# Sample attention of a decoder layer: two phases in a row against eight steps side by side

## The chip, the core and the metric

The program runs on one core of a Trainium2 chip. Five engines work there from queues of their own and meet at semaphores: TensorE (PE in the rows, and PEld for its weight loads) multiplies, VectorE (DVE) and ScalarE (ACT) work on what lies in the on-chip memories, GpSimd (POOL) subtracts here, and SyncE (SP) starts most transfers. The metric is the device time of one execution in microseconds (us), as the median over runs. The kernel before takes 1402.89 us (median of 3 runs, 1401.07 to 1404.97).

## The reference

One layer of a decoder: an input projection, two kinds of mixing, an output projection and a layer norm. There are 512 prompt tokens, and 8 samples with 4 new tokens each, behind 1024 cached positions. Cached keys and values lie in pages of 128 positions, 8 pages for a sample, 512 KB a page and kind. What matters here, cut from the reference (L is 1028, topk 256, 8 heads of width 128):

```python
def _sample_attention(l, q, k_new, v_new, qi, ki_new, wi, cache_k, cache_v, cache_kidx, page_table):
    ...
    _, idx = lax.top_k(scores, topk)
    valid = idx <= qpos[None, :, None]
    ...
    k_sel = jnp.where(is_past, cache_k[l, phys_page, offset].astype(k_new.dtype), k_new[bidx, nidx])
    v_sel = jnp.where(is_past, cache_v[l, phys_page, offset].astype(v_new.dtype), v_new[bidx, nidx])
    return _sparse_attend(q, k_sel, v_sel, valid)

def _pool_mix(u_ext, n_hist, w_pool, pool_scale):
    # trailing means over 2, 4, 8, 16 tokens minus the token, for four groups of 256 channels,
    # then a 256 x 256 map for each group
    ...
def _combine(x, a, p, ga, gb, w_out, ln_g, ln_b):
    mixed = jnp.concatenate([a.reshape(B, T, ATTN_WIDTH) * jax.nn.silu(ga),
                             p * jax.nn.silu(gb)], axis=-1)
    h = (DEEPNORM_ALPHA * x + jnp.einsum('btc,cd->btd', mixed, w_out)).astype(jnp.float32)
    ...
```

The kernels read every page and put a mask over the scores in place of the gather: positions that were not picked get -1e30 ahead of the softmax.

## The kernel before

The kernel runs through stages A (indexer), C (attention of the prompt, head by head), B (attention of the samples, and pooling) and D (output projection and norm). The change lies in stage B, lines 788 to 870 (ScalarE), 1122 to 1281 (TensorE), 1549 to 1632 (VectorE) and the transfers in `group` on SyncE (lines 445 to 516). Stages A, C and D stay as they are.

**Tiles and quarters.** A projection turns 2048 inputs into 128 output columns for 544 tokens. Such a tile is two units of weights (512 KB each), and a unit is two quarters: `quarter` is 24 matmuls on line 922, six for each of four chunks of inputs (high and low parts of weights and activations). Weights land in `rawW`, ScalarE rounds them into `wH` (`high`), GpSimd takes the difference into `wL` (line 558). Two accumulators in PSUM, `acc0` and `acc1`, take turns from tile to tile, so that a finished tile is copied out while the next one is computed. Stage B has four groups, and each has four tiles (two for the pooling input U, two for its gate) and two samples, a and b.

**One sample.** First the keys: in 16 steps `turned(n)` transposes four 128 by 128 blocks of key pages into bank 4 or 5 (line 1139), VectorE (even n, line 1562) or ScalarE (odd n, line 593) copies them into `kPT`, and `products(n)` multiplies them by the sample's queries (line 1155), two heads side by side in two of the four 32-column strips of the array. Three quarters stand between those steps. Then come the new keys, two quarters, and the transposes of the probabilities (lines 1186 and 1189) once the softmax is through on VectorE and ScalarE. Then the values: `value_pages` takes the eight pages in two lots of four (line 1200, eight heads in four strips), with a quarter between, and after the last quarter the output is turned (line 1230). When both samples are done, the map of the pooling group follows (line 1280).

**What sets the order.** All queues are written out by hand and each runs strictly in its order. Bank use is a table: `Banks.stage` deals names out over banks in turn, and a use waits until the one before it in the same bank was read. Bank 4 and 5 serve keys, probabilities, history rows, outputs and the pooling map; banks 6 and 7 serve scores and the value sums. `vPage` has 4 slots of one page, and SyncE starts a page's transfer when TensorE has freed its slot (`v_free`). `kPage` has 2 slots of two pages. SyncE's order in a group is: pooling inputs, weights, key pages, two value pages, weights, key pages, mask, two value pages, weights, and the other four value pages behind one another.

## Time and profile before

| what | value |
|---|---|
| median of 3 runs | 1402.89 us (1401.07 to 1404.97) |
| profiled execution: its time, its span | 1407.33 us, 1405.5 us |
| TensorE busy | 1281.5 us, 91% of the span |
| VectorE, ScalarE, GpSimd busy | 587.0, 361.7 and 350.6 us (42%, 26%, 25%) |
| matmuls of the projections (line 922) | 7008 records, 508.6 + 491.9 + 491.9 us |
| stage B | 690.0 to 1173.6 us |
| stage D | from 1176.0 us |
| granted TensorE clock over the span | 0.955 of 2.4 GHz |
| DMA over the span | 170.67 MB, mean 121 GB/s |

The profile shows one execution. Busy times of TensorE add up the records, which overlap, so that a start-to-start distance in the timeline says more than a record's duration. "Idle before" names what ended a wait. Line numbers are those of the kernel that was run.

### The profile page before, as it was taken

How to read it: one execution, taken by the hardware profiler on the slowest of the kernel's cores; microseconds unless marked ns; L12 is line 12 of the kernel's file. 1: busy time of each engine (PE TensorE's matmuls, PEld its weight loads, DVE VectorE, ACT ScalarE, POOL GpSimd, SP SyncE). 2: the span in 40 equal slices, each digit the busy share in tenths (PEclk: the TensorE clock that was granted, in tenths of full speed). 3: DMA queues.
4: the chain of work that ended last, by engine and by line, in shares of the span. 5: the costliest groups of instructions: out<-in, count | busy, mean ns of one | idle time of the engine just before them, and what ended most of it. 6: DMA issues, size and time to landing. Idle time of an engine off the chain costs nothing. (4 is left out here: it accounts for less than half of the span.)

```text
span 1405.5 us, 27397 instructions
## 1 busy us (share of the span) xinstructions
PE 1281.5 (91%) x10300; PEld 1128.3 (80%) x10300; DVE 587.0 (42%) x1079; ACT 361.7 (26%) x663; POOL 350.6 (25%) x150
## 2 busy tenths in 40 slices
PE   7899968898999999899898998988989898999995
PEld 6777758898999999899776767757677677999993
DVE  3555588973084066137431323313132234222226
ACT  4223231223223123223321222212222123212210
POOL 2322202422433243243211212202120121434320
PEclk9999978999999999999999999999999999999996
DMA  8423121322332233234247465464736646422203
GB/s 245 115 72 82 33 73 54 85 78 60 91 98 69 73 102 83 62 92 121 86 147 263 160 198 180 141 219 142 245 121 195 212 140 200 137 83 81 88 2 128
DMA packets 197987, 170.67 MB, mean 121 GB/s; under 512 B 19890, under 2 KB 178538, under 8 KB 196658
## 3 DMA queue, kind: packets, MB, share of 16 engines
q1 hardware_dynamic: 184458, 160.48, 37.3%
q10 hardware_dynamic: 13424, 8.67, 2.2%
q8 instruction: 80, 1.31, 0.4%
q14 instruction: 25, 0.20, 0.0%
HBM read 159.47 MB, written 9.74 MB: 120 GB/s over the span
## 5 line engine op out<-in xcount | busy, mean ns | idle before, releaser
L558 POOL TENSOR_TENSOR wL<-rawW,wH 128x1024 fp32r<-128x1024 f32 (+1 forms) x146 | 350.4, 2401 | 1006.6 <-ACT wH L579 1006.6
L922 PE MATMUL acc<-actH,wH 128*128 128x272 f32 (+1 forms) x2336 | 508.6, 300 | 11.6 <-issue 8.2
L922 PE MATMUL acc<-actH,wL 128*128 128x272 f32 (+1 forms) x2336 | 491.9, 293 | 0.0
L922 PE MATMUL acc<-actL,wH 128*128 128x272 f32 (+1 forms) x2336 | 491.9, 293 | 0.0
L922 PEld LDWEIGHTS acc<-actH,wH 128*128 128x128 f32 (+1 forms) x2336 | 375.5, 193 | 37.4 <-issue 35.4
L922 PEld LDWEIGHTS acc<-actL,wH 128*128 128x128 f32 (+1 forms) x2336 | 376.9, 193 | 0.0
L922 PEld LDWEIGHTS acc<-actH,wL 128*128 128x128 f32 (+1 forms) x2336 | 373.6, 193 | 0.0
L579 ACT ACTIVATE wH<-rawW 128x1024 fp32r<-128x1024 f32 (+1 forms) x146 | 153.9, 1055 | 300.3 <-PE acc L922 278.0
L1562 DVE COPY kPT<-bank 128x512 f32<-128x512 f32 x64 | 44.2, 691 | 176.3 <-PE bank L1139 176.3
L1139 PEld LDWEIGHTS bank<-sq,kPage 128*128 128x128 f32 x512 | 56.0, 144 | 53.9 <-issue 50.5
L1155 PE MATMUL bank<-kPT,qPad 128*32 128x256 f32 x512 | 81.9, 399 | 13.0 <-DVE kPT L1562 6.6
L1139 PE MATMUL bank<-sq,kPage 128*128 128x128 f32 x512 | 85.5, 293 | 5.0 <-issue 5.0
L593 ACT ACTIVATE kPT<-bank 128x512 f32<-128x512 f32 x64 | 38.2, 597 | 140.3 <-PE bank L1139 139.6
L1653 DVE SCALAR_TENSOR_TENSOR y<-y,bank 128x512 f32 x16 | 11.0, 688 | 135.0 <-PE bank L1290 125.9
L1484 DVE SCALAR_TENSOR_TENSOR gate<-tanhC,raw 128x544 f32<-128x544 f32 x8 | 5.8, 723 | 144.7 <-ACT raw L770 144.7
L1384 DVE SCALAR_TENSOR_TENSOR scoreP<-relu,wiN,scoreP 128x256 f32<-128x256 f32 (+2 forms) x54 | 38.8, 753 | 63.9 <-ACT relu L636 63.9
L1200 PE MATMUL bank<-vPage,probST 128*4 128x128 f32 x1024 | 35.9, 276 | 23.3 <-DMA vPage<-in_cache_v 23.3
L1622 DVE SCALAR_TENSOR_TENSOR mixed<-bank,gateS 128x32 f32 x8 | 1.5, 192 | 129.2 <-PE bank L1230 129.2
L636 ACT ACTIVATE relu<-bank 128x512 f32<-128x512 f32 (+3 forms) x63 | 29.2, 504 | 87.5 <-PE bank L979 71.9
L1200 PEld LDWEIGHTS bank<-vPage,probST 128*4 128x4 f32 x1024 | 23.5, 87 | 33.1 <-DMA vPage<-in_cache_v 30.3
L1155 PEld LDWEIGHTS bank<-kPT,qPad 128*32 128x32 f32 x512 | 18.8, 109 | 38.4 <-issue 25.5
L979 PE MATMUL bank<-kiT,raw 64*128 64x256 f32 (+2 forms) x108 | 32.0, 587 | 15.3 <-DVE qiN L1398 11.7
(193 smaller groups left out, 988.4 us busy)
## 6 DMA issues: line engine op xcount, KB each, us to landing
rawW<-in_w_in SPq DMA_DIRECT2D x112, 512.0 KB, 3.8
kPage<-in_cache_k SPq DMA_DIRECT2D x64, 512.0 KB, 5.2
vPage<-in_cache_v SPq DMA_DIRECT2D x64, 512.0 KB, 5.2
rawW<-in_w_out SPq DMA_DIRECT2D x32, 512.0 KB, 3.9
y<-in_x_prompt SPq DMA_DIRECT2D x4, 1024.0 KB, 8.1
out_y_prompt<-y SPq DMA_DIRECT2D x8, 512.0 KB, 2.8
xnat<-in_x_prompt SPq DMA_DIRECT2D x2, 1024.0 KB, 7.7
xnat<-in_x_prompt ACTq DMA_DIRECT2D x2, 1024.0 KB, 11.3
```

The lines of the kernel that those rows point to most:

```text
L558: pool.tensor_tensor(wL[:, slot, :, 0:width], rawW[:, slot, :, 0:width], wH[:, slot, :, 0:width].bitcast(F32), ALU.subtract).then_inc(stag ...
L579: act.activation(wH[:, t.slot, :, 0:width], rawW[:, t.slot, :, 0:width], ACT.Copy).then_inc(high_ready[t.slot], 1)
L593: act.activation(dst, src, ACT.Copy).then_inc(bank_free[b.slot], 1)
L636: act.activation(relu[0:rows, t.slot, 0:n], src[0:rows, 0:n], ACT.Relu).then_inc(relu_full[t.slot], 1)
L922: last = pe.matmul(acc[t.slot][0:width, e, 0:HT], w[:, u.slot, k, 0:width], a[:, kk, e * HT:(e + 1) * HT], start=(kk == 0 and w is wH and ...
L979: full(b, pe.matmul(take(b)[:, 0:(t + 1) * P], raw[part, slot, t * P:(t + 1) * P], kiT[part, 0:(t + 1) * P], start=True, stop=True))
L1139: last = pe.transpose(dst[:, (2 * e + a) * P:(2 * e + a + 1) * P], kPage[:, 1 - k.slot, a, 2 * hp + e, :], ident)
L1155: last = pe.matmul(bank[st.slot][at:at + SPAN, pair % 2 * 256:pair % 2 * 256 + 256], qPad[:, X, h * NS:(h + 1) * NS], kPT[:, n % 2, e, :], ...
L1200: return pe.matmul(bank[o.slot][j * SPAN:j * SPAN + NT, a * P:(a + 1) * P], probs, values, start=start and a == 0, stop=stop and a == HALF ...
L1384: dve.scalar_tensor_tensor(sc, relu[:, r.slot, 0:(t + 1) * P], wiN[:, t - 1, ds(h, 1)], sc, ALU.mult, ALU.add).then_inc(bank_free[b.slot], 1)
L1562: dve.tensor_copy(kPT[:, 0, :, :].rearrange("p h k -> p (h k)"), bank_wait(dve, b)[:]).then_inc(bank_free[b.slot], 1)
L1653: dve.scalar_tensor_tensor(at, at, ALPHA, bank_wait(dve, b)[:].rearrange("p (t c) -> p t c", t=TT), ALU.mult, ALU.add).then_inc(bank_free[ ...
```

## The change

Stage B becomes a pipeline over samples. A sample's eight value pages run beside the next sample's keys in eight steps, m = 0 to 7. In step m TensorE transposes the keys of step m + 1 (eight blocks, banks 4 and 5), may run a quarter, multiplies the keys of step m (four heads in four strips, `key_products`), and takes value page m of the sample before (`value_page`). Pieces:

- The keys of the first sample run ahead of the loop with quarters 0 to 4. The loop runs three times over two samples, "b" beside the values of "a", and "c" (the next group's "a") beside the values of "b". The last group is written out behind it, and its last eight value pages have no keys beside them.
- All tiles of the stage use `acc1` (`tile_turn`). The two halves of `acc0` become banks: OUT (8) for the sums over values, SIDE (9) for history rows, last rows, new keys, the third part of the probabilities, outputs and the pooling map. In the rows a wait on them is bank_free8 and bank_free9.
- Transposed keys have a second place, two rows of `mixed` that are still unused then (`key_slot`). The output is copied into `probST` instead of `probS`, so the mask of the next sample can be loaded after the probabilities are turned.
- SyncE starts each value page four steps ahead and each pair of key pages three steps ahead; two more tiles of output weights are loaded within the last group instead of behind it.
- On VectorE the window sums (line 1591), gates and pooling results are cut up and stand between the key copies. On ScalarE the copies of projections, `high` and the last rows do.

The diff, cut: bank tables, SyncE's order, TensorE's order, and for the first sample of a group the orders of ScalarE and of VectorE.

```diff
+def tile_turn(tile, i=None, per=0):
+    if tile < TILE_B:
+        slot, n, step = tile % 2, tile // 2, per // 2
+    elif tile < TILE_D:
+        slot, n, step = 1, TILE_B // 2 + tile - TILE_B, per
+    else:
+        slot, n, step = (tile - TILE_D) % 2, (tile - TILE_D) // 2, per // 2
+        n += TILE_B // 2 + (KC if slot else 1)
+    return Turn(slot, n if i is None else i * step + n)
...
-            outS = probS[:, 0:HALF * P].rearrange("p (a d) -> p a d", a=HALF)
+            outS = probST[:].rearrange("p a t -> p (a t)").rearrange("p (a d) -> p a d", a=HALF)
+            def key_slot(n):
+                if n // 2 % 2:
+                    return mixed[:, KC - 2 + n % 2, 0:4 * P]
+                return kPT[:, n % 2, :, :].rearrange("p h k -> p (h k)")
...
+        OUT, SIDE = 8, 9
+        bank[OUT], bank[SIDE] = acc[0][:, 0, :], acc[0][:, 1, :]
...
+        def beside_keys(X, Y):
+            return [*key_uses(Y, 0, 2), f"Pt0{X}", f"Pt1{X}", *key_uses(Y, 2, 16)]
+        side = ["h0", "Pt2a", "h1", "u0", "u1", "Snb", "OTa", "Pt2b", "m0p", "m0s", "m1p", "m1s"]
+        LOOPS = GROUPS - 1
+        stages = []
+        for names in ((key_uses("a"), ["S0a", "S1a"], ["Sna"], []),
+                      (beside_keys("a", "b") + beside_keys("b", "c"), ["S0b", "S1b", "S0c", "S1c"],
+                       [*side, "Snc", "OTb"], ["Oa", "Ob"]),
+                      (beside_keys("a", "b") + ["Pt0b", "Pt1b"], ["S0b", "S1b"], [*side, "OTb"], ["Oa", "Ob"])):
+            times = LOOPS if len(stages) == 1 else 1
+            stages.append([banks.stage(n, w, times) for n, w in zip(names, ((4, 5), (6, 7), (SIDE,), (OUT,)))])
...
+                mask(1, "Pt2a", g)
+                for m in range(PAGES):
+                    if m % 2 == 0:
+                        unit(8 + m // 2, last, g)
+                        if m < 4 or not last:
+                            key_pages(1 + m // 4, (m // 2 + 2) % 4, f"K{2 * m + 3}b", g)
+                    value_page((m + 4) // 8, (m + 4) % 8, g)
                 if not last:
-                    for pair in range(2):
-                        key_pages(g + 1, 0, pair)
-            with sp.Fori(0, GROUPS - 1) as g:
+                    mask(2, "Pt2b", g)
+                for m in range(PAGES):
+                    if m % 2 == 0:
+                        unit(12 + m // 2, last, g)
+                        if not last:
+                            key_pages(2 + m // 4, (m // 2 + 2) % 4, f"K{2 * m + 3}c", g)
+                    if m < 4 or not last:
+                        value_page(1 + (m + 4) // 8, (m + 4) % 8, g)
+                    if m == 5 and not last:
+                        pool_loads(1, g)
...
+                for j in range(QUARTERS):
+                    h = QUARTERS * (m % 2) + j
+                    keys = key_slot(2 * m + j // 2)[:, j % 2 * 2 * P:(j % 2 + 1) * 2 * P]
+                    last = pe.matmul(bank[st.slot][j * SPAN:(j + 1) * SPAN, pair % 2 * 256:pair % 2 * 256 + 256],
+                                     qPad[:, x % 2, h * NS:(h + 1) * NS], keys,
+                                     start=(h < QUARTERS), stop=(h >= QUARTERS))
...
+            keys_turned("a", 0)
+            for m in range(8):
+                if m + 1 < 8:
+                    keys_turned("a", m + 1)
+                if m in (0, 2, 4, 5):
+                    quarter((0, 0, 1, 1, 2, 3)[m])
+                key_products("a", m)
+            new_keys("a")
+            quarter(4)
...
+                keys_turned("b", 0, g)
+                history(0)
+                quarter(5, g)
+                probs_turned("a")
+                quarter(6, g)
+                history(1)
+                for m in range(PAGES):
+                    if m + 1 < 8:
+                        keys_turned("b", m + 1, g)
+                    if m in (0, 2, 3, 4, 5):
+                        quarter((7, 0, 8, 9, 10, 11)[m], g)
+                    if m == 1:
                         last_rows(0)
-                    probs_turned(X)
-                    quarter(X, 5)
-                    value_pages(X, 0, 4)
-                    quarter(X, 6)
-                    value_pages(X, 4, 8)
-                    quarter(X, 7)
-                    output_turned(X)
-                pe.wait_ge(pooled_ready, 2 * g + 4)
-                pe.wait_ge(wp_in, 16 * g + 16)
-                for e in range(2):
-                    for part, values in (("p", U[:, :, HIST:HIST + NP_]), ("s", pooledS[:])):
-                        b = bb(f"m{e}{part}", g)
-                        dst = take(b)
-                        n = values.shape[-1]
-                        for c in range(2):
-                            last = pe.matmul(dst[:, 0:n], wp[:, c, e * P:(e + 1) * P], values[:, c, :],
-                                             start=(c == 0), stop=(c == 1))
-                        full(b, last)
+                    if m == 3:
+                        last_rows(1)
+                    key_products("b", m, g)
+                    value_page("a", m)
+                new_keys("b", g)
+                quarter(12, g)
+                output_turned("a")
+                if not last:
+                    keys_turned("c", 0, g)
+                quarter(13, g)
+                probs_turned("b")
+                quarter(14, g)
+                for m in range(PAGES):
+                    if not last and m + 1 < 8:
+                        keys_turned("c", m + 1, g)
+                    if m == 0:
+                        quarter(15, g)
+                    elif m in (2, 3, 4, 5) and not last:
+                        quarter(14 + m, g)
+                    if m in (1, 2, 3, 4):
+                        pool_mix((m - 1) // 2, "ps"[(m - 1) % 2])
+                    if not last:
+                        key_products("c", m, g)
+                    value_page("b", m)
+                if not last:
+                    new_keys("c", g)
+                    quarter(20, g)
+                output_turned("b")
+            with pe.Fori(0, LOOPS) as g:
+                group(g, False)
+            group(LOOPS, True)
...
+                key_copied("b", 0, g)
+                history(0)
+                probs_copied("a")
+                history(1)
+                key_copied("b", 1, g)
+                key_copied("b", 2, g)
+                copy_tile(1, g)
+                high(TILE_B + 3, 0, g, 4)
+                last_rows(0)
+                key_copied("b", 3, g)
+                high(TILE_B + 3, 1, g, 4)
+                key_copied("b", 4, g)
+                last_rows(1)
+                key_copied("b", 5, g)
+                high(TILE_B + 4, 0, g, 4)
+                key_copied("b", 6, g)
+                key_copied("b", 7, g)
+                copy_tile(2, g)
+                high(TILE_B + 4, 1, g, 4)
+                out_copied("a")
+                exps(2 * g + 1)
...
+                key_copied("b", 0, g)
+                queries(1, g)
+                key_copied("b", 1, g)
+                pool_levels(0, 0, 2)
+                key_copied("b", 2, g)
+                pool_levels(0, 2, 4)
+                key_copied("b", 3, g)
+                pool_end(0)
+                key_copied("b", 4, g)
+                pool_levels(1, 0, 2)
+                key_copied("b", 5, g)
+                masked("b", 0, g)
+                pool_levels(1, 2, 4)
+                key_copied("b", 6, g)
+                pool_end(1)
+                key_copied("b", 7, g)
+                softmax_end("b", g)
+                gated("a")
```

How the order changes on TensorE. First the key steps. kPage holds key pages as loaded, kPT and mixed transposed keys, qPad the queries, vPage value pages; line 1139 becomes 1217, 1155 becomes 1234 and 1200 becomes 1285. Before, in the middle of a sample's keys:

```order
L1155 MATMUL bank7<-kPT,qPad 32x256 [waits bank_free4]
L1155 MATMUL bank7<-kPT,qPad 32x256
L1139 MATMUL bank4<-sq,kPage 128x128 [waits bank_free4]
L1139 MATMUL bank4<-sq,kPage 128x128 x3
L1155 MATMUL bank7<-kPT,qPad 32x256 [waits bank_free5]
L1155 MATMUL bank7<-kPT,qPad 32x256
```

Now, in step m = 6 (the whole of it, without a quarter):

```order
L1217 MATMUL bank4<-sq,kPage 128x128 [waits bank_free4]
L1217 MATMUL bank4<-sq,kPage 128x128 x3
L1217 MATMUL bank5<-sq,kPage 128x128 [waits bank_free5]
L1217 MATMUL bank5<-sq,kPage 128x128 x3
L1234 MATMUL bank7<-kPT,qPad 32x256 [waits bank_free5,bank_free4]
L1234 MATMUL bank7<-kPT,qPad 32x256 x3
L1285 MATMUL acc0<-vPage,probST 4x128 [waits v_in2]
L1285 MATMUL acc0<-vPage,probST 4x128 x7
```

Eight blocks are transposed in a row, four heads are multiplied in a row, and one value page follows, where four blocks and two heads took turns before and all value pages stood behind the keys.

Second, the probabilities of a sample on TensorE. Lines 1186 and 1189 become 1271 and 1274. Before, and then now:

```order
L1186 MATMUL bank4<-sq,probS 128x128 [waits bank_free4,probS_ready]
L1186 MATMUL bank4<-sq,probS 128x128 x3
L1186 MATMUL bank5<-sq,probS 128x128 [waits bank_free5]
L1186 MATMUL bank5<-sq,probS 128x128 x3
L930 REGISTER_ALU
L1189 MATMUL bank4<-sq,probS 32x128 [waits bank_free4]
```

```order
L1271 MATMUL bank4<-sq,probS 128x128 [waits bank_free4,probS_ready]
L1271 MATMUL bank4<-sq,probS 128x128 x3
L1271 MATMUL bank5<-sq,probS 128x128 [waits bank_free5]
L1271 MATMUL bank5<-sq,probS 128x128 x3
L1011 REGISTER_ALU
L1274 MATMUL acc0<-sq,probS 32x128 [waits bank_free9]
```

The last part had to wait for the first in bank 4 to be copied out, and goes to the SIDE bank now.

Third, ScalarE around the copy of the second projection tile. Line 593 becomes 632 (key copies out of bank 5), 813 to 816 become 846 to 849 (the tile's copies into U), 579 becomes 618 (`high`) and 850 becomes 837 (the exponentials). Before, the rows at the end of a sample's keys, and then now, in steps 0 to 2:

```order
L593 ACTIVATE U<-bank4 128x8x15 [waits pooled_ready]
L593 ACTIVATE kPT<-bank5 128x512 [waits bank_full5] x2
L850 ACTIVATE probS,stat<-probS,stat 128x1056 [waits max_ready]
L585 REGISTER_ALU
L350 REGISTER_ALU [waits tile_ready1]
L813 ACTIVATE U<-acc1 128x272 [waits bank_full5]
L814 ACTIVATE U<-acc1 128x240
L815 ACTIVATE newU<-acc1 128x32
```

```order
L632 ACTIVATE mixed<-bank5 128x512 [waits bank_full5]
L632 ACTIVATE kPT<-bank5 128x512 [waits bank_full5]
L846 ACTIVATE U<-acc1 128x272 [waits tile_ready1]
L847 ACTIVATE U<-acc1 128x240
L848 ACTIVATE newU<-acc1 128x32
L849 ACTIVATE U<-acc1 128x8x4
L618 ACTIVATE wH<-rawW 128x1024 [waits stage_free0,w_landed0]
```

The tile was copied after all the keys and the exponentials. Now it is copied between the keys of step 2 and of step 3, and the next tile's first quarter, in the same accumulator, waits for it.

## Rows read from the trace of the kernel before

**Rows 1.** Stretches: length; busy PE, PEld, DVE, ACT, POOL; clock; DMA share; GB/s.
```profile
690.00:813.20 123.20, 108.37 (x1006) 82.47 (x1004) 34.91 (x64) 27.27 (x55) 19.60 (x9) 0.96 0.57 188
813.20:931.40 118.20, 106.87 (x1004) 81.33 (x1004) 33.40 (x61) 27.07 (x54) 19.55 (x8) 0.97 0.56 185
931.40:1053.40 122.00, 109.97 (x1004) 83.64 (x1004) 33.46 (x61) 27.07 (x54) 19.52 (x8) 0.94 0.55 179
1053.40:1173.60 120.20, 108.39 (x1004) 83.05 (x1004) 33.32 (x61) 27.07 (x54) 19.50 (x8) 0.96 0.51 164
```

**Rows 2.** TensorE's waits in 690 to 1175 us: total, times, longest.
```profile
PE bank L1200 <- DMA vPage<-in_cache_v: 23.3, 24, 2.1
PE bank L1155 <- DVE kPT L1562: 6.6, 7, 4.2
PE bank L1155 <- ACT kPT L593: 5.3, 4, 1.4
PE bank L1139 <- issue: 5.0, 3, 1.8
PE bank L1189 <- ACT probST L593: 4.8, 4, 1.5
PE bank L1280 <- DVE mixed L1631: 3.2, 4, 0.8
```

**Rows 3.** Timeline of TensorE, key steps: start, us, line, count.
```profile
695.28 0.63 PE L1155 MATMUL bank<-kPT,qPad 128*32 128x256 f32 x4 [4.24 <-DVE kPT L1562]
...
703.76 0.66 PE L1139 MATMUL bank<-sq,kPage 128*128 128x128 f32 x4
704.35 0.63 PE L1155 MATMUL bank<-kPT,qPad 128*32 128x256 f32 x4
704.91 0.65 PE L1139 MATMUL bank<-sq,kPage 128*128 128x128 f32 x4
...
707.19 0.66 PE L1139 MATMUL bank<-sq,kPage 128*128 128x128 f32 x4
707.60 0.50 PE L922 MATMUL acc<-actH,wH 128*128 128x272 f32 x2
```

**Rows 4.** Timeline of TensorE, value pages of the first sample.
```profile
735.88 1.93 PE L1200 MATMUL bank<-vPage,probST 128*4 128x128 f32 x64
737.74 0.52 PE L922 MATMUL acc<-actH,wH 128*128 128x272 f32 x2
```

**Rows 5.** Stretches at a stop of TensorE; columns as in rows 1.
```profile
718.60:723.40 4.80, 4.67 (x49) 2.32 (x48) 1.30 (x3) 1.47 (x3) 0.00 (x0) 1.00 0.29 85
745.00:750.00 5.00, 4.27 (x57) 3.27 (x58) 0.00 (x0) 0.38 (x1) 0.00 (x0) 0.70 1.00 383
```

**Rows 6.** Timeline of TensorE at the end of the stage.
```profile
1171.28 1.99 PE L1280 MATMUL bank<-U,wp 128*128 128x512 f32 x4 [0.79 <-DVE mixed L1631]
1173.10 0.53 PE L1280 MATMUL bank<-pooledS,wp 128*128 128x32 f32 x4
1175.99 0.49 PE L922 MATMUL acc<-actH,wH 128*128 128x272 f32 x2 [2.36 <-DVE actL L1640]
```

**Rows 7.** Timeline of ScalarE: a tile copied, high, a key copy.
```profile
753.66 0.40 ACT L813 ACTIVATE U<-acc 128x272 f32<-128x272 f32 x1 [5.35 <-PE acc L922]
...
754.36 1.08 ACT L579 ACTIVATE wH<-rawW 128x1024 fp32r<-128x1024 f32 x1
755.30 0.62 ACT L593 ACTIVATE kPT<-bank 128x512 f32<-128x512 f32 x1
```

**Rows 8.** VectorE's window sums in the stage: count, busy us, mean ns.
```profile
L1591 DVE SCALAR_TENSOR_TENSOR win<-win,wtab 128x676 f32<-128x676 f32 (+2 forms) x24 | 37.8, 1576 | 2.2 <-DVE win L1591 0.6
```

**Rows 9.** Transfers in 690 to 1174 us: KB each, us to landing.
```profile
vPage<-in_cache_v SPq DMA_DIRECT2D x64, 512.0 KB, 5.2
```

**Rows 10.** Timeline of TensorE where the loop before turns back.
```profile
342.87 0.51 PE L922 MATMUL acc<-actH,wH 128*128 128x272 f32 x2 [2.66 <-issue]
```

**Rows 11.** The chain that ended last, one output tile.
```profile
1196.36 12.02 PE acc L922 x96
```

More of the change, by code:

```diff
@@ L925, in unit @@
                 if 1 in quarters:
[L926 removed]
+                    last.then_inc(tile_ready[t.slot] if half else stage_free[u.slot // 2], 1)
             def take(b):
@@ L1170, in new_keys, with quarter, keys_turned @@
+            def quarter(n, g=None):
+                unit(TILE_B + n // 4, n // 2 % 2, g, 4, quarters=(n % 2,))
+            def keys_turned(X, m, g=None):
+                k = turn(4 * "abc".index(X) + m // 2, 2, g, 8)
+                if m % 2 == 0:
+                    pe.wait_ge(k_in[k.slot], 32 * k.full)
+                for n in (2 * m, 2 * m + 1):
+                    b = bb(f"K{n}{X}", g)
                     dst = take(b)
[L1171 to L1174 removed]
+                    for e in range(2):
+                        for a in range(2):
+                            last = pe.transpose(dst[:, (2 * e + a) * P:(2 * e + a + 1) * P],
+                                                kPage[:, 1 - k.slot, a, 2 * (n % 4) + e, :], ident)
@@ new lines, in new_keys @@
+            def new_keys(X, g=None):
+                b = bb(f"Sn{X}", g)
+                dst = take(b)
+                for h in range(H):
+                    at = h % QUARTERS * SPAN
+                    last = pe.matmul(dst[at:at + SPAN, 0:NS], qPad[:, "abc".index(X) % 2, h * NS:(h + 1) * NS], kS[:, h, :],
+                                     start=(h < QUARTERS), stop=(h >= QUARTERS))
+                full(b, last)
+            copied(TILE_C + 31)
+            keys_turned("a", 0)
[5 more added lines that the diff above has]
+                key_products("a", m)
```

565 lines of the change are left out of this document (292 added, 273 removed).

## Prediction

> **What bounds the kernel now.** I read the stretches first, one for each of the four groups of the stage [rows 1]: 120.9 us in the mean, TensorE busy for 88 to 90%, VectorE, ScalarE and GpSimd for under a third, the transfer engines 0.51 to 0.57 busy. So TensorE sets the time, and it is neither full nor at full clock (0.94 to 0.97). Next TensorE's waits in the stage [rows 2]: 48.2 us in all, nearly half of them for value pages, the rest for copied keys, the last part of the probabilities, the pooling results and "issue", which stands three times at a loop's turn. The timeline then shows what a key step costs though nothing waits [rows 3]: 703.76 to 704.91 is one n, four transposes and two heads, 1.15 us. Four transposes alone take 0.41 us (707.19 to 707.60). So 0.59 - 0.41 = 0.18 us is lost between transposes and products, and products with the way back take 0.56 us. The value pages, eight heads in four strips, take 1.86 us for four pages or 0.465 each, as long as they have landed [rows 4]; the last ones come late, up to 2.1 us each [rows 2]. Last the clock around such a stop [rows 5]: in the five us behind one it was 0.70, that is, at 1.2 GHz in place of 2.4 for about 60% of them, where a stretch without a stop shows 1.00.
>
> **The change part by part.** It is summed against the profiled execution (1407.33 us, its span 1405.5 us), which was 4.4 us above the median of 1402.89.
>
> *Key steps.* Two n cost 2.30 us before. Now one step holds eight transposes (0.82), one gap (0.18), and four heads in four strips. What these four take, the trace does not show for keys. If all four strips run at once, they take what two heads took, 0.56 with the way back: the step is 1.56 and saves 0.74. If strips run only in pairs, the second pair adds its work without the way back, 0.56 less a gap of 0.13 to 0.18, about 0.4, and the step saves 0.3. I take the first, because the value rows show four strips at once: a matmul of 512 columns takes 1.82 / 4 = 0.455 us a record [rows 6], so one of 128 takes 0.114; sixteen of them in a row would be 1.8 us, and a value page took 0.465 [rows 4]. With 64 steps: **-47.4 us** (lower end -20).
>
> For four strips, the page "TensorE: Matmul & The Clock Gate" of the Trainium skill (section "Part 3: Packing small matmuls") gives 2.38 times for three column tiles, 79% of ideal. Its figure would make products of four heads about 0.1 us longer a step and the result 7 us higher; the value page of this trace is nearer to ideal, 1.8 / 0.465 = 3.9 times, and the sum goes by that.
>
> *Value pages.* Their 0.465 us stays, but each now stands between products and transposes and not behind another page. The extra gap lies between 0 and 0.18 us [rows 3]; I take 0.12, nearer to the gap seen: **+7.7 us** (0 to +11.5).
>
> *Waits that go.* Value pages are started four steps ahead. A step without a quarter is about 1.56 + 0.465 + 0.12 = 2.15 us, one with a quarter (24 of the 96 matmuls in 12.02 us, so 3.0 us [rows 11]) 5.2 us. Four steps are at least 10 us, and a page lands 5.2 us after its issue [rows 9]. Key pages come three steps ahead with about the same room. So the 23.3 us go. The waits for copied keys go too, but for the 4.2 us at the very start [rows 3], since a copy now has most of a step and two places: 2.4 + 5.3. The third part of the probabilities has a bank of its own (4.8), and pooling maps stand a step apart (3.2). Together **-39.0 us** (lower end -25, if copies between other work give a third back). The "issue" waits were 5.0 us for three turns of the loop; in the loop of stage C one is 2.66 [rows 10], and the new loop turns back twice: 5.3, so **+0.3**.
>
> *Clock.* Over the four stretches (1 - clock) x length is 4.9 + 3.5 + 7.3 + 4.8 = 20.6 us lost [rows 1]. It fell after stops. The stop at the start stays and the tail gets a new one, each about 1.5 to 1.7 us (five us at 0.70 [rows 5]): **-17.2 us** (lower end 0, if it falls in the new mix as well).
>
> *What is added.* With one accumulator, a tile's first quarter waits for ScalarE to copy the tile before. Of the eight such places in two groups the tightest is step 2: behind quarter 7 come 4.3 us of other TensorE work, and ScalarE has to copy key 2 (due 2.0 us behind that quarter, 0.62 long), then the tile (0.70 from its first copy to the next instruction [rows 7]), and is through at some 3.4. Ahead of quarter 12 it is 5.2 against some 3.5. Cost nothing; if it were late, quarter, products and value page queue behind it. In the first sample ScalarE copies a tile and rounds weights (0.94 to the next instruction [rows 7]) ahead of the last key, 2.4 us against 2.1: **+0.3**. VectorE's window sums of 1.58 us each [rows 8], two in a row at most, fall in the 5.3 us between one bank 4 of keys and the next where a quarter stands; nothing. SyncE waits in its order for a value page's slot, then starts weights and keys; it is paced by TensorE and its backlog is at most six transfers (3 MB). At 188 GB/s for 0.57 of the time [rows 1] that is 330 GB/s, so 9.5 us.
>
> *Tail.* The last eight value pages have no keys beside them. From the end of quarter 15: page 0 at 0.5 us, pages 1 to 3 at 2.8, 4.2 and 6.6 us (pooling maps between, each waiting for VectorE to read the one SIDE bank). Page 7 starts loading at 6.9 and lands 5.2 us or a little more later [rows 9]. With the new keys' part, copy, turn, gate and the first chunk of stage D, 3.8 us more, stage D starts at 16. Of these 16 about 9 are work that was in the old sum; 7.6 are idle, where the old end had 2.4 [rows 6]. **+5.2 us** (+2 to +8). The added output weights load in that time, and stage D had no other stop on TensorE.
>
> *Sum.* -47.4 + 7.7 - 39.0 + 0.3 - 17.2 + 0.3 + 5.2 = -90.1 us, so 1407.3 - 90.1 = 1317.2, less the 4.4 us between this execution and the median: **1313 us**.
>
> **Rivals.**
>
> *A, strips in pairs.* Products of four heads take two turns: 64 x 0.42 = 27 us back, 1340 us. Before, two heads ran at once at most, which speaks neither way; the value rows speak against.
>
> *B, pages still late.* 86.6 MB must come in about 390 us, 220 GB/s and two thirds of the 330 above, where 179 in the mean did before. For it: value, key and weight transfers now overlap all the time, and weights come in short pieces. If the 23.3 us stay and the clock falls after them as before: 1313 + 23 + 17 = 1353 us.
>
> *C, copies late.* VectorE and ScalarE have 16 key copies a sample between sums, gates and tiles, each in strict order. If each sample has 3 us of such waits: 1313 + 24 = 1337 us. For it: before, 5.3 us were lost to ScalarE with far less between its copies [rows 2]. Against: both are under a third busy.
>
> *D, clock falls between quarters, once a sample.* Steps 6 and 7 and the new keys are 5.2 us without a quarter, where the longest such stretch so far, 718.6 to 723.4, kept 1.00 [rows 5]. If it falls each time, 8 x 1.7 = 14 us: 1327 us.
>
> *E, slower.* The clock stays at 1.2 GHz wherever no quarter runs. Outside the 64 quarters (193 us) the new stage has some 200 us; at half clock throughout they cost 200 more. From 45% of them on, the 90 us are eaten. At 60% it is 1313 + 120 = 1433 us, slower than before. Against it: the same kinds of instructions at 1.00 in rows 5.
>
> The same page of the Trainium skill (section "Part 4: PE-mode transpose") says that a transpose doesn't count as busy for the clock gate. By that rule, D or E would come about, since eight transposes now stand in a row. The 4.8 us at 1.00 in rows 5, a third of them transposes, don't bear it out.
>
> **How the numbers follow.** My forecast 0.58 with a range of its own of 1302 to 1328; A 0.10, B 0.09, C 0.12, D 0.06, E 0.05. The range of 1300 to 1345 holds nearly all of the forecast and D and most of A and C, some 8 in 10; B and E lie above, and copies, gaps and tail that come out better than taken below. Faster by over 0.3% (4.2 us, about what a measurement of this kernel can tell from no change): 0.94; within it 0.01, which is what the far end of B leaves; slower 0.05.
>
> **What would show it.** Right: the stage lasts 385 to 400 us and a loop pass some 93 to 98; a step without a quarter 2.1 to 2.3 us and the four heads' products with their way on under 0.6; no wait for value pages but in the last four; clock 0.98 or more until the tail; TensorE idle for about 7 to 8 us between quarter 15 and stage D; stage D unchanged at 229 us. Wrong: products of 0.9 us or more (A), TensorE waiting for value or key pages within the loop (B), waits for key copies or for acc_copied beyond 10 us in all (C), a clock under 0.96 in the loop (D, E).

## The result: 1297.37 us, and the profile after

| | before | after |
|---|---|---|
| median of 4 runs each, us | 1403.49 (1401.07 to 1404.97) | 1297.37 (1295.51 to 1298.31) |
| ratio, 95% interval | 1 | 0.924 (0.9226 to 0.9261) |
| profiled execution, us | 1407.33 | 1295.51 |
| stage of samples in it, first key transpose to stage D, us | 690.0 to 1176.0: 486.0 | 686.6 to 1064.3: 377.7 |

The kernel is 106 us faster, 16 more than forecast and 2.6 below the range. Measured twice more, beside a kernel before that took 1406.8 and 1409.1 us, the ratio was 0.9223 (0.9197 to 0.925) and 0.9231 (0.9203 to 0.926). Between the two profiled executions lie 111.8 us: 108.3 in the stage, 3.4 ahead of it, where the code is the same. Stage D is unchanged, 229.5 us before and 229.4 after.

The first view after is the table of stretches, which answers to [rows 1]: the start with the first two samples, twice the length of a loop pass (from one place in a pass to the same in the next), the last group up to its last quarter, and the tail behind it. Columns are those of rows 1.

```profile
686.60:771.20 84.60, 80.23 (x829) 71.15 (x828) 33.84 (x61) 23.80 (x51) 14.34 (x7) 0.98 0.76 248
771.20:863.60 92.40, 89.25 (x1006) 77.79 (x1005) 33.33 (x60) 26.20 (x54) 19.08 (x8) 1.00 0.71 236
863.60:955.70 92.10, 89.10 (x1006) 77.72 (x1005) 33.33 (x60) 26.20 (x54) 19.07 (x8) 1.00 0.70 237
955.70:1047.00 91.30, 91.30 (x1028) 80.01 (x1030) 34.36 (x58) 25.62 (x54) 19.06 (x8) 1.00 0.67 222
1047.00:1064.30 17.30, 11.92 (x162) 5.84 (x155) 3.77 (x8) 4.93 (x8) 4.67 (x2) 0.80 0.73 218
```

Two samples take 92 us in place of 121, TensorE is busy for 97% of the loop and throughout the last group, its clock is at the full 2.4 GHz there, and the transfer engines run evenly at 0.7 where they had 0.51 to 0.57. Time lost to the clock, (1 - clock) x length, is 1.7 us at the start and 3.5 in the tail, against 20.6.

Next TensorE's waits in the stage, which answer to [rows 2]: total, times, longest.

```profile
PE bank L1217 <- issue: 5.4, 2, 3.0
PE bank L1217 <- DVE kPT L1667: 4.1, 1, 4.1
PE acc L1285 <- DMA vPage<-in_cache_v: 2.3, 2, 1.9
PE acc L1003 <- DVE actL L1815: 1.8, 1, 1.8
PE acc L1003 <- issue: 0.8, 1, 0.8
PE acc L1339 <- DVE mixed L1748: 0.7, 2, 0.4
PE acc L1314 <- issue: 0.5, 1, 0.5
PE bank L1234 <- ACT mixed L632: 0.3, 1, 0.3
```

Before, the same list had the 48.2 us of [rows 2], 0.6 for a history row and 2.4 at the start of stage D [rows 6], 51.2 in all; now it has 15.9, with the 1.8 at the start of stage D. Of the 24 waits for value pages two are left, both in the tail; there is no wait for an accumulator, and 0.3 us for a copied key beyond the one at the start.

Then the timeline of TensorE, which answers to [rows 3, 4]. The first four rows are a step with a quarter (its own rows left out), which stands between transposes and products. The last four are a step without one: products (L1234), value page (L1285), transposes (L1217), and round again.

```profile
745.67 0.62 PE L1285 MATMUL acc<-vPage,probST 128*4 128x128 f32 x16
746.22 1.09 PE L1217 MATMUL bank<-sq,kPage 128*128 128x128 f32 x8
...
750.24 0.64 PE L1234 MATMUL bank<-kPT,qPad 128*32 128x256 f32 x8
750.70 0.62 PE L1285 MATMUL acc<-vPage,probST 128*4 128x128 f32 x16
...
755.27 0.64 PE L1234 MATMUL bank<-mixed,qPad 128*32 128x256 f32 x8
755.73 0.62 PE L1285 MATMUL acc<-vPage,probST 128*4 128x128 f32 x16
756.28 1.09 PE L1217 MATMUL bank<-sq,kPage 128*128 128x128 f32 x8
757.30 0.64 PE L1234 MATMUL bank<-kPT,qPad 128*32 128x256 f32 x8
```

From 755.27 to 757.30 a step is 2.03 us: products 0.46, value page 0.55 with the way to the transposes, transposes 1.02 with the way to the products. Four heads in four strips thus take 0.46 us, where eight matmuls of 256 columns in a row would take 1.82 at the rate of [rows 6]: 4.0 times. The page "TensorE: Matmul & The Clock Gate" of the Trainium skill (section "Part 3: Packing small matmuls") has 2.38 times for three column tiles; this trace shows more. A step with a quarter takes 5.03 us (745.67 to 750.70), 3.00 more, which is what 24 such matmuls take in a row [rows 11]: the gap between transposes and products stays, and stands around the quarter.

Last the tail on TensorE, which answers to [rows 6]; lines of quarters are left out. L1339 are pooling maps, L1314 the output's turn.

```profile
1040.66 0.27 PE L1274 MATMUL acc<-sq,probS 128*32 128x128 f32 x1
...
1046.88 0.62 PE L1285 MATMUL acc<-vPage,probST 128*4 128x128 f32 x16
1047.43 1.99 PE L1339 MATMUL acc<-U,wp 128*128 128x512 f32 x4
...
1054.91 1.06 PE L1285 MATMUL acc<-vPage,probST 128*4 128x128 f32 x32
1057.83 1.03 PE L1285 MATMUL acc<-vPage,probST 128*4 128x128 f32 x16 [1.87 <-DMA vPage<-in_cache_v]
1059.30 1.03 PE L1285 MATMUL acc<-vPage,probST 128*4 128x128 f32 x16 [0.43 <-DMA vPage<-in_cache_v]
...
1061.84 0.66 PE L1314 MATMUL acc<-sq,probST 128*128 128x128 f32 x2 [0.55 <-issue]
```

Quarter 15 ends at 1046.9 and stage D starts at 1064.3, 17.4 us later. Page 7 is the last to land. From page 6 on the work runs at half clock, which shows in rows of 1.03 us where they were 0.62.

### The profile page after: what moved, and what is told of

Its sections match the earlier page's. It is cut to its first block, busy times and chain, and to the rows that moved or that the text cites. A ratio compares the mean times of both kernels' runs of the same rounds, so it can differ in the third digit from the quotient of the medians.

```text
span 1293.7 us, 27396 instructions
## 1 busy us (share of the span) xinstructions
PE 1203.6 (93%) x10300; PEld 1104.7 (85%) x10300; DVE 589.1 (46%) x1079; ACT 358.1 (28%) x663; POOL 348.5 (27%) x150
## 4 chain that ended last, share of the span: by engine, by line
PE 75%; DVE 12%; issue 8%; ACT 2%; DMA 2%; DVEq 0%; ACTq 0%; SPq 0%
PE acc L1003 55%; PE bank L1217 5%; PE bank L1234 3%; PE acc L1285 2%; PE bank L1060 2%; DVE scoreP L1534 2%; DVE top L1530 2%; PE bank L1163 2%; PE bank L1144 1%; PE acc L1339 1%; DVE rot L1461 1%; DVE top L1569 1%; DVE scoreS L1572 1%; DVE y L1872 1%; DMA xnat<-in_x_prompt 1%
## 5 line engine op out<-in xcount | busy, mean ns | idle before, releaser
L1003 PE MATMUL acc<-actH,wH 128*128 128x272 f32 (+1 forms) x2336 | 503.4, 297 | 11.7 <-issue 8.7
L1003 PEld LDWEIGHTS acc<-actL,wH 128*128 128x128 f32 (+1 forms) x2336 | 371.7, 191 | 0.0
L1217 PE MATMUL bank<-sq,kPage 128*128 128x128 f32 x512 | 69.9, 280 | 9.5 <-issue 5.4
L1217 PEld LDWEIGHTS bank<-sq,kPage 128*128 128x128 f32 x512 | 56.0, 142 | 21.9 <-issue 16.8
L1667 DVE COPY mixed<-bank 128x512 f32<-128x512 f32 x32 | 22.1, 692 | 92.5 <-PE bank L1217 92.1
L632 ACT ACTIVATE kPT<-bank 128x512 f32<-128x512 f32 x32 | 19.1, 598 | 105.9 <-PE bank L1217 105.3
L1667 DVE COPY kPT<-bank 128x512 f32<-128x512 f32 x32 | 22.1, 691 | 53.5 <-PE bank L1217 52.8
L632 ACT ACTIVATE mixed<-bank 128x512 f32<-128x512 f32 x32 | 19.2, 599 | 85.0 <-PE bank L1217 79.0
L1285 PE MATMUL acc<-vPage,probST 128*4 128x128 f32 x1024 | 40.3, 277 | 2.3 <-DMA vPage<-in_cache_v 2.3
L1569 DVE MAX8 top<-scoreS 32x8 f32<-32x1056 f32 x32 | 39.9, 1247 | 2.9
L1285 PEld LDWEIGHTS acc<-vPage,probST 128*4 128x4 f32 x1024 | 26.9, 88 | 16.2 <-DMA vPage<-in_cache_v 3.1
```

Of the source, the lines that this page charges most:

```text
L632: act.activation(dst, src, ACT.Copy).then_inc(bank_free[b.slot], 1)
L1003: last = pe.matmul(acc[t.slot][0:width, e, 0:HT], w[:, u.slot, k, 0:width], a[:, kk, e * HT:(e + 1) * HT], start=(kk == 0 and w is wH and ...
L1217: last = pe.transpose(dst[:, (2 * e + a) * P:(2 * e + a + 1) * P], kPage[:, 1 - k.slot, a, 2 * (n % 4) + e, :], ident)
L1285: return pe.matmul(bank[o.slot][j * SPAN:j * SPAN + NT, a * P:(a + 1) * P], probs, values, start=start and a == 0, stop=stop and a == HALF ...
L1569: own.step(dve.max(top, scores))
L1667: dve.tensor_copy(key_slot(2 * m), bank_wait(dve, b)[:]).then_inc(bank_free[b.slot], 1)
```

## The experiments

Ratios are to the kernel before, run beside each kernel on one chip; "stage" is the length, in the profiled execution, that was 486.0 before and 377.7 after.

**The changed kernel again**, as the reference of the second and third set of runs.

> The changed kernel as it is, beside the three others of this call. All theories: 0.924 of the time of the kernel before (interval so far 0.9226 to 0.9261), about 106 us less.

> The changed kernel as it is, for the runs beside it: 0.922 to 0.925 of the kernel before, as twice already.

1297.75 and 1298.90 us, ratios 0.9223 and 0.9231, stages 377.7 and 377.1 us. The three ratios agree.

**Pairs of heads (e1_pairs).** The changed kernel with the old key step: four transposes, two heads, twice a step.

The edit, shortened (in `key_products`, then in the loop of steps, which now turns the first four there):

```diff
                 for j in range(QUARTERS):
+                    if j == 2 and m + 1 < 8:
+                        keys_turned(X, m + 1, g, (1,))
                     h = QUARTERS * (m % 2) + j
...
-                        keys_turned("b", m + 1, g)
+                        keys_turned("b", m + 1, g, (0,))
```

> The changed kernel with the key steps in the old alternation: in 7 of a sample's 8 steps four transposes, two heads, four transposes, two heads; value pages stay beside the keys. Theory (four heads at once in four strips and one handing-over in place of two are worth 2.30 - 1.56 = 0.74 us a step): 56 steps, +41 us, 1338 us, and up to 8 us more if copies come late. Rival (the gain came from waits and clock, the order of heads hardly matters): under +15 us, below 1312 us.

1340.26 us, ratio 0.950 (0.9463 to 0.9537): 38 us more than the changed kernel by the ratios; stage 421.3, 43.6 more. The theory's 1338 us came. A step without a quarter on TensorE:

```profile
764.12 0.63 PE L1236 MATMUL bank<-mixed,qPad 128*32 128x256 f32 x4
764.67 0.65 PE L1217 MATMUL bank<-sq,kPage 128*128 128x128 f32 x4
765.26 0.41 PE L1236 MATMUL bank<-mixed,qPad 128*32 128x256 f32 x2
765.27 0.50 PE L1287 MATMUL acc<-vPage,probST 128*4 128x128 f32 x6
...
766.25 0.66 PE L1217 MATMUL bank<-sq,kPage 128*128 128x128 f32 x4
766.84 0.62 PE L1236 MATMUL bank<-kPT,qPad 128*32 128x256 f32 x4
```

From products to products, 764.12 to 766.84, it is 2.72 us, where the changed kernel has 2.03; a step with a quarter takes 5.73 (758.39 to 764.12) and not 5.03. So an altered step costs 0.70 more, and 56 of them 39 us. The clock (8.1 us lost and not 5.3) and later value pages in the tail (3.9 us and not 2.3) make up the rest of the 43.6. No wait for a key page or value page stands in the loop. So the order of the key step is worth 39 us for 56 steps within the pipeline.

**Value pages in lots of four (e2_lots).** The changed kernel with pages 0 to 3 behind step 3 and 4 to 7 behind step 7.

The edit, which stands for "b" as well:

```diff
-    value_page("a", m)
+    if m in (3, 7):
+        for p in range(m - 3, m + 1):
+            value_page("a", p)
```

> The changed kernel with each sample's value pages in two lots of four, behind steps 3 and 7, and the transfers in SyncE's order as they are. Theory (what counts is that pages are started far enough ahead, not that each stands alone; the second lot is issued about 12 us before its use): the pages cost no wait, key pages behind them in SyncE's order may be 1 to 2 us late in each sample, so +0 to +16 us, 1297 to 1313 us, and the clock stays above 0.98 in the loop. Rival (one page in each step is what removes waits and keeps the clock): +35 us or more, 1332 us.

1361.81 us, ratio 0.967 (0.9642 to 0.9697), stage 440.5: some 60 us given back, where none or up to 16 were expected. The theory failed, and the rival's 35 us or more came. TensorE's waits and SyncE's for a value slot, then SyncE's issues and TensorE at one place:

```profile
PE bank L1217 <- DMA kPage<-in_cache_k: 33.9, 7, 5.8
PE acc L1285 <- DMA vPage<-in_cache_v: 6.9, 4, 3.8
SPq L426 <- PE acc L1285: 172.0, 15, 16.1
```

```profile
798.60 0.38 SPq L405 DMA_DIRECT2D rawW<-in_w_in  x1
800.64 0.85 SPq L426 DMA_DIRECT2D kPage<-in_cache_k  x2
```

```profile
801.88 0.64 PE L1234 MATMUL bank<-kPT,qPad 128*32 128x256 f32 x8
806.93 1.97 PE L1217 MATMUL bank<-sq,kPage 128*128 128x128 f32 x8 [4.42 <-DMA kPage<-in_cache_k]
```

SyncE issues in one order, and over 690 to 1123 us it waits 172 us for value slots, up to 16.1 at a time. While it waits for a value slot, the key pages behind it wait too; they are issued at 800.64 and wanted at 802.5. The changed kernel's SyncE waits for value slots 42 times, 12.4 us at the longest, and TensorE waits for no key page in the stage. The clock, 0.93 over 690 to 1123 us, fell too: 34.1 us were lost to it in the stage, against 5.3. So in this kernel it is the even pace of slots, one a step, that keeps the transfers early. Late pages with the clock behind them are what rival B feared, but here they come from the order of one queue and not from the transfer rate.

**Half the value transfers (e3_before_half).** The kernel before without the transfers of pages 4 to 7; products use pages 0 to 3 again, so half of the values is left out.

The edit, shortened (TensorE's waits and slot releases change to match):

```diff
 def value_page(X, p):
-    t = turn(8 * X + p, 4, g, 16)
+    if p >= 4:
+        return
+    t = turn(4 * X + p, 4, g, 8)
...
```

> The kernel before without the transfers of value pages 4 to 7 of each sample: the products of pages 4 to 7 read the pages 0 to 3 once more (the attention of the samples is computed from half of the values). All else stays. It prices the late value pages with all that hangs on them. Theory (a wait costs 0.19 us more than its row shows, since the row counts from the modelled end of the matmul before, so 23.3 + 24 x 0.19 = 27.9 us, and the clock gives some 15 us): 1403.5 - 43 = 1360 us. Rival (what the prediction took, 23.3 us and a clock that fell for other reasons too): 1375 us or more.

1361.04 us, ratio 0.965 (0.9622 to 0.9678): 48 us less by the medians; stage 445.6, 40.4 less. The theory's 1360 us came. No wait for vPage is left, the others stay to within 0.7 us. The clock:

```profile
690.00:1136.00 446.00, 416.71 (x4023) 321.21 (x4022) 136.67 (x248) 109.90 (x220) 78.77 (x33) 0.98 0.48 156
```

By this rounded mean 0.02 x 446 = 8.9 us were lost; the clock's record in the trace, summed, gives 6.8, and 20.5 for the kernel before. Waits 23.3 and clock 13.7 make 37.0 of the 40.4. So the clock adds more than half of their wait to the price of late value pages. Nearly all of the rest, 3.8 us, is hidden in the rows themselves. The timeline of the kernel before shows it:

```profile
742.33 0.62 PE L1200 MATMUL bank<-vPage,probST 128*4 128x128 f32 x16 [0.77 <-DMA vPage<-in_cache_v]
745.09 0.62 PE L1200 MATMUL bank<-vPage,probST 128*4 128x128 f32 x16 [2.13 <-DMA vPage<-in_cache_v]
```

From start to start it is 2.76 us, less the page's own 0.465 [rows 4] 2.30; the row says 2.13, because it counts from the modelled end of the matmuls before. 24 times 0.16 are 3.8 us. The sum over all value pages bears it out: start to start, without wait rows and clock, they took 38.3 us before and 34.1 here.

**The key step alone (e5_before_order).** The kernel before with eight transposes, then four heads, and two more key places in mixed.

```diff
...
-for n in range(16):
-    if n + 1 < 16:
-        turned(n + 1)
-    beside(n)
-    products(n)
+for n in range(0, 16, 2):
+    if n + 2 < 16:
+        turned(n + 2)
+        turned(n + 3)
+    beside(n + 1)
+    products(n)
+    products(n + 1)
```

> The kernel before, with only the order of a key step changed: eight transposes, then four heads' products, with two more places for copied keys in the last two rows of mixed; samples and value pages stay as they were. Theory (one hand-over less for two n and four strips at once, nothing else): 64 steps x 0.745 us = 48 us less, 0.966 of the time before; the step alone is then 1.56 us. Rival 1 (a hand-over of 0.12 us comes on top, as the forecast had it for value pages): 40 us less, 0.972. Rival 2 (key pages late): a pair of key pages is then wanted every 3.1 us without a quarter, where 1 MB at the 330 GB/s of before takes 3.2; TensorE waits for kPage and gives 10 to 25 us back, 0.975 to 0.985. The waits for value pages stay (23 us).

1381.25 us, ratio 0.982 (0.9782 to 0.9856): 25.5 us less; stage 462.8, 23.2 less. Rival 2 of the expectation came. One step on TensorE, its waits, and the stretch:

```profile
819.11 1.09 PE L1145 MATMUL bank<-sq,kPage 128*128 128x128 f32 x8
820.13 0.64 PE L1161 MATMUL bank<-kPT,qPad 128*32 128x256 f32 x8
820.71 1.09 PE L1145 MATMUL bank<-sq,kPage 128*128 128x128 f32 x8
```

```profile
PE bank L1209 <- DMA vPage<-in_cache_v: 21.5, 24, 1.7
PE bank L1145 <- DMA kPage<-in_cache_k: 10.1, 7, 3.2
```

```profile
690.00:1151.00 461.00, 405.10 (x4008) 333.02 (x4008) 135.40 (x243) 110.19 (x219) 78.21 (x32) 0.92 0.57 188
```

The step is 1.60 us, so 64 x 0.70 = 45 us went. Back came 10.1 us of late key pages and 0.08 x 461 = 36.9 us of clock (37.5 by its record) against 20.5, some 17 more. 45 - 10 - 17 = 18, and waits for copies and value pages are 5.6 us smaller: some 24, against 23.2 measured. The new order alone wants keys faster than they are brought and stops more often, and the granted clock falls at the stops. The next run speaks against the eight transposes in a row as the cause.

**Both (e6_order_half).** The two edits together, half of the values left out again.

> The kernel before with the new key step of the run beside it and also without the transfers of value pages 4 to 7 (the products use pages 0 to 3 again, so half of the values is left out). Theory: the two halves of the gain add up, 48 for the step and 48 for late value pages with the clock after them: 96 us less, 0.932 of the time before. What is then missing to the changed kernel, some 10 us, is the other waits that went (copied keys, probabilities, pooling) less its longer tail. Rival: they overlap (key pages late in the one, or the clock's loss counted in both), and the pair gives under 80 us, over 0.943.

1333.03 us, ratio 0.947 (0.9444 to 0.9501): 74 us less, stage 416.4. That is what the two gave singly (25.5 + 47.6), so they add, but not to the 96 of the theory: the rival's number, under 80, came, as the key pages stay late (11.1 us, 5 times). The clock cost 10.2 us here, with the same transposes in a row as in e5, where it cost 37.5: the stops for value pages made that difference. Neither part nor both (stage 69.6 us shorter) reach the 108.3 us of the pipeline, which brings every page and has no key page late.

**A value page's price in its place (e9_one_page).** The changed kernel without the products of value pages 1 to 7 in the loop, 42 of 64.

```diff
-                    for h in range(H):
-                        end = products(h, probST[:, p, column(h)], vPage[:, v.slot, h, :], p == 0, False)
-                    end.then_inc(v_free[v.slot], 1)
+                    if p == 0 or isinstance(g, int):
+                        for h in range(H):
+                            end = products(h, probST[:, p, column(h)], vPage[:, v.slot, h, :], p == 0, False)
+                        end.then_inc(v_free[v.slot], 1)
+                    else:
+                        pe.sem_inc(v_free[v.slot], 1)
```

> The changed kernel without the products of value pages 1 to 7 in the loop's three passes (42 of 64 pages; all transfers and waits stay). What a value page costs in its place between products and transposes. Theory (a hand-over moves with the page, none is added): 42 x 0.465 = 19.5 us less than the changed kernel, 0.910 of before, and a step without quarter takes 1.6 us. Forecast's term (0.12 us extra for each page): 42 x 0.585 = 24.6 us less, 0.906, step 1.44. Rival: the pages are cover for the transfers and the copies; without them key pages or copied keys come late, TensorE's waits for kPage, kPT or mixed show it, and under 12 us are gained, over 0.915.

1281.80 us, ratio 0.911 (0.9077 to 0.9136): 17.1 us less than the changed kernel beside it; stage 361.1, 16.1 less. The parts of a step on TensorE, with nothing between products and transposes:

```profile
746.71 0.64 PE L1234 MATMUL bank<-mixed,qPad 128*32 128x256 f32 x8
747.28 1.09 PE L1217 MATMUL bank<-sq,kPage 128*128 128x128 f32 x8
...
756.47 1.09 PE L1217 MATMUL bank<-sq,kPage 128*128 128x128 f32 x8
757.49 0.64 PE L1234 MATMUL bank<-kPT,qPad 128*32 128x256 f32 x8
```

Products with the way back take 0.57 us here and transposes 1.02, so the step is 1.59, and 2.03 with the page: 0.44 us a page, 18.5 for 42. Against the changed kernel beside it, waits for copied keys grew by 1.2 us, those for value pages in the tail by 0.9 and the clock's loss by 0.4, while the stops at the loop's turns were 1.2 shorter. That makes 17.2 of the 16.1 measured, so 1 us is open. The 24.6 us of the forecast's term (ratio 0.906) are outside the interval; the theory's 0.910 is inside.

**The tail (e4_tail, e7_tail2, e8_tail3).** In e4 the last sample's pages 0 to 3 stand ahead of quarter 15.

```diff
 quarter(14, g)
+if last:
+    for p in range(4):
+        value_page("b", p)
...
-                    value_page("b", m)
+                    if not last or m >= 4:
+                        value_page("b", m)
```

> The changed kernel with the last sample's value pages 0 to 3 ahead of quarter 15 in place of behind it, so that pages 4 to 7 start loading about 4 us (page 4) to 8 us (page 7) earlier. Theory (the end is set by page 7's landing, 4.4 us of the 17.4 between quarter 15 and stage D are waits for it): 4 to 6 us less, 1292 us. Rival (the chain of pooling results in the one SIDE bank and the low clock set the end): within 2 us of 1297.

1295.93 us, ratio 0.920 (0.9155 to 0.924). From the turn of the probabilities to stage D it took 20.8 us in place of 23.7 (1040.66 to 1064.32). No page is late, the pooling maps are instead (2.3 us). The stage as a whole was 377.7, no shorter: what stands ahead of the tail was 3 us longer, with a clock of 0.91 around a loop turn. The time is within 2 us of the changed kernel's, as the rival had it, but the ratio is lower by 0.005 with overlapping intervals, so the gain in time is undecided. In e7 the first two maps go ahead of pages 0 and 2, and each gate is followed by its pooling outputs.

> The changed kernel with the end of its last sample put in another order: value pages 0 to 3 and the first two pooling maps ahead of quarter 15, so that the slots of pages 4 to 7 come free earlier, and each gate followed at once by its two pooling outputs on VectorE. In the earlier run with the pages alone moved, TensorE waited 2.3 us for VectorE between pooling maps and no longer for a page. Theory: the tail is a chain of loads and of one bank that the four pooling maps share; with both taken out it loses 6 us for the pages and 2 more for the maps, 8 to 9 us less than the changed kernel (0.918 of the kernel before). Rival: the tail is set by ScalarE's copies and the output's turn behind quarter 15, which stay: then no more than the 6 us of the earlier run.

1296.29 us, ratio 0.922 (0.9197 to 0.925), tail 23.5: nothing gained. The theory's 8 to 9 us did not come, nor any of the 6 that the rival allowed. The four last pages land 7.8 us after their issue in the median, against 4.2 in the changed kernel, and TensorE waits for the last two until 1057.5 and 1059.0. In e8 pages 0 to 3 come first, then two maps, quarter 15 and the rest, and SyncE starts pages 4 to 7 ahead of the output weights.

```diff
-                    if m % 2 == 0:
+                    if m % 2 == 0 and not (last and m == 2):
+                        if last and m == 4:
+                            unit(13, last, g)
...
```

> The changed kernel with its end in a third order: value pages 0 to 3 of the last sample straight behind quarter 14, then two pooling maps, quarter 15, pages 4 to 7 with the other two maps between; SyncE starts those four pages ahead of the next output weights; each gate is followed at once by its two pooling outputs. Measured so far from the turn of the last probabilities to stage D: 23.6 us in the changed kernel, 20.8 with pages 0 to 3 moved, 23.5 with the maps ahead of the pages (page 6 landed 6.8 us after its issue, with weights in the same queue). Theory (the tail is set by the landing of pages 4 to 7, then by the shared bank of the maps): 18 to 19.5 us here, so the kernel takes 4 to 5 us less than the changed one, 0.919 to 0.920 of before. Rival (ScalarE's copies of tile 3 and of the output and the first chunk of stage D set it): 20.5 to 21, as with the pages alone, 3 us less.

1295.98 us, ratio 0.920 (0.9171 to 0.9223). SyncE's issues and TensorE at the end:

```profile
1050.50 3.79 SPq L426 DMA_DIRECT2D vPage<-in_cache_v  x4
1054.44 11.08 SPq L405 DMA_DIRECT2D rawW<-in_w_out  x3
```

```profile
1046.47 0.27 PE L1276 MATMUL acc<-sq,probS 128*32 128x128 f32 x1
...
1061.51 1.06 PE L1287 MATMUL acc<-vPage,probST 128*4 128x128 f32 x32
...
1065.89 0.57 PE L1005 MATMUL acc<-actH,wH 128*128 128x272 f32 x2 [1.82 <-DVE actL L1824]
```

19.4 us from the turn to stage D, within the 18 to 19.5 of the theory. The changed kernel has 23.7 in its first profiled execution and 22.7 in the one beside this run, so it is 3.3 to 4.2 shorter. Its stage is 375.5 us, 1.6 below the changed kernel beside it, and the medians differ by 2.9, the rival's 3 and not the theory's 4 to 5. The shorter tail is shown by the trace; that the kernel is faster is likely, but the intervals of the two ratios overlap.

## Why the prediction was right in direction and too small

By the forecast's own terms, against the stage's 108.3 us:

| term | forecast | measured |
|---|---|---|
| key steps | -47.4 | -45 (step alone 1.60 in e5) |
| value pages' extra gap | +7.7 | -2 (0.44 us a page in e9, not 0.465 + 0.12) |
| TensorE's wait rows, with loop, accumulator and tail | -33.2 | -35.3 (51.2 to 15.9) |
| clock, by its record | -17.2 | -15.2 (20.5 to 5.3) |
| not in the sum | | -10.8 |

*The step that failed* is "Value pages. Their 0.465 us stays, but each now stands between products and transposes"; the 0.12 us on top was wrong. The key step of 1.56 already held products "with the way back", 0.56. A value page behind the products takes over that way back, and does not add one: 2.03 us in the trace where the forecast had 2.15. That is 0.12 for each of the 56 pages that stand so, about 7 us of the 7.7 that the term added, and e9 shows it by taking pages away. It is more than the 2.6 us by which the time lies below the range.

*What the sum did not have.* It is of about the same size, so the failed step is not the whole of the error. Start to start, without wait rows and without (1 - clock) x length, the stage took 414.3 us before and 356.6 after, 57.7 less, where the forecast's first two rows have 39.7:

| on TensorE, us | before | after |
|---|---|---|
| key transposes | 70.7 | 56.5 |
| key products | 70.0 | 29.9 |
| value pages and new values | 38.3 | 38.0 |
| quarters | 198.7 | 200.2 |
| all else | 36.6 | 32.1 |

Key steps and value pages have 47 of the 57.7. Wait rows count from a modelled end, so each of 24 late pages had cost 0.16 us more than its row: 3.8. "All else" gives 4.5, of which 2.0 are the transposes of the probabilities and 1.5 the new keys, which the forecast left as they were. Some 2.4 us stay open. The 3.4 us ahead of the stage are no part of the change.

*Key steps, right.* Four strips run at once. Rival A did not come: products of four heads took 0.46 us, not 0.9. That it named 1340 us and e1 took 1340.26 is chance, as A adds 27 to 1313 and e1 adds 43 to 1297.

*Waits, right.* The value pages' waits are gone from the loop, and e3 shows that they and the clock behind them were worth 40 to 48 us, where the forecast had 40.5 for the two. "Key pages come three steps ahead with about the same room" was true only of the pipeline: e5 and e2 lose 10 and 34 us to them. Rivals B and C did not come: no page is late in the loop, and key copies cost 0.3 us beyond the start.

*Clock, right.* 1.00 throughout the loop of the profiled execution, against D and E. In the 13 traces, 64 stretches at half clock begin within the stage, and each begins during a stop of TensorE or at most 1.5 us after one; none stands behind transposes alone. The same page of the Trainium skill (section "Part 4: PE-mode transpose") says that transposes don't count as busy in the same way for the clock gate; with eight in a row, half of each step without a quarter, no row here shows a fall.

*Tail, nearly right.* 17.4 us and not 16, of which 5.4 idle and not 7.6: page 6 waits 1.87 us and page 7 0.43, and the clock is at 0.80 over it. That pages are late there, and the clock with them, was forecast. Of the signs named ahead, clock, waits and stage D came; stage, loop pass and step were each a little shorter than named (377.7 us, 92 and 2.03), and so was TensorE's idle time in the tail.

## What to carry to other kernels

Look at the hand-overs between kinds of matmuls as a cycle: here a value page put between two kinds moved the gap and added none. A stop of TensorE costs its row, a little more that the row hides, and clock on top, so a late page is worth more than its wait. How much clock varies: 13.7 us with 23.3 us of waits in e3, 17 more with 10 us more of late key pages in e5, and 29 more with 34 in e2. A faster step alone can turn half its gain into late pages and a lower clock, as in e5; what let this change keep it is one free slot a step, which paces a queue that issues in order.

## What the runs showed that was not expected

- Where the new loop turns, TensorE stood still for 2.2 us (e4) to 3.8 us (e9), in the changed kernel 2.3 to 3.0. The clock sometimes fell there and sometimes did not: over 780 to 820 us it was 1.00 in the changed kernel, 0.96 in its second profiled execution and 0.91 in e4, with the same instructions. That is 3.6 us between executions.
- Freeing slots earlier does not by itself make the next pages land earlier: in e7 the last four were issued 1.3 to 2.6 us sooner after the turn of the probabilities and landed 7.8 us after their issue in the median, against 4.2 in the changed kernel. In both, one tile of weights is issued between them, so that is not the difference; what is was not shown.
- Strips of the value page run beside the last pair of heads (e1, 765.26 and 765.27), so matmuls of different kinds overlap when their strips are free.
